# Two of eight token tiles of an expert mixture move from dense matmuls to gathered rows

## The reference

```python
experts = (i1 * PEER_NKEYS + i2).reshape(T, PEER_HEADS * K)
gates = jax.nn.softmax(top_s, axis=-1).reshape(T, PEER_HEADS * K)
...
a = jax.nn.gelu(jnp.einsum('td,ted->te', xb, u_tab[eb]), approximate=False)
coeff = (gb * a.astype(jnp.float32)).astype(xb.dtype)
return jnp.einsum('te,ted->td', coeff, v_tab[eb])
```

## Time and profile before

| what | value |
|---|---|
| median of three runs | 3731.43 us |
| span of the profiled execution | 3732.1 us |
| start of sweep 1, of sweep 2 (first matmuls) | 775.3, 2321.6 us |
| TensorE busy | 3570.5 us (96%) |
| DVE, ACT, POOL busy | 2290.6, 1202.6, 520.4 us |
| moved by DMA | 556.75 MB |

### The profile page before, as it was taken

How to read it: one execution, slowest core, us unless ns; L and a number is a source line. 1 busy time by engine, 2 the same in 40 slices (tenths; PEclk the granted TensorE clock), 3 DMA queues, 4 the chain that set the end, 5 groups by cost and what they waited for, 6 DMA issues and landing times. The chain is left out here.

```text
span 3732.1 us, 47838 instructions
## 1 busy us (share of the span) xinstructions
PE 3570.5 (96%) x16504; PEld 2955.7 (79%) x16504; DVE 2290.6 (61%) x3828; ACT 1202.6 (32%) x1342; POOL 520.4 (14%) x277
## 2 busy tenths in 40 slices
PE   4984999989999999999999999999999999999998
PEld 3862687878888888888888887888888878888887
DVE  5336243578988888888888844444444454444444
ACT  3123342123333333333333333222222232222222
POOL 0000000022333333333323332000000010000000
PEclk9995599999999999999999999999999999999999
DMA  6400022223333333333333333656655565565563
GB/s 245 157 27 23 15 105 90 84 72 141 135 141 139 140 140 137 138 140 135 136 139 136 138 132 138 235 190 198 242 188 192 196 209 191 188 199 188 189 198 139
DMA packets 223303, 556.75 MB, mean 149 GB/s; under 512 B 16528, under 2 KB 105744, under 8 KB 221072
## 3 DMA queue, kind: packets, MB, share of 16 engines
q1 hardware_dynamic: 222384, 552.88, 42.0%
q0 software_dynamic: 864, 3.15, 0.2%
HBM read 404.96 MB, written 150.99 MB: 149 GB/s over the span
## 5 line engine op out<-in xcount | busy, mean ns | idle before, releaser
L77 DVE TENSOR_TENSOR v_lo<-v_raw,v_hi 128x1024 fp32r<-128x1024 f32 x256 | 317.1, 1239 | 763.6 <-ACT v_hi L72 763.6
L1318 POOL TENSOR_TENSOR onehot<-onehot,slots 128x1024 fp32r<-128x1024 f32 x256 | 482.7, 1906 | 1349.5 <-DVE onehot L1378 1349.5
L1622 PE MATMUL y_ps<-v_hi,c_hi 128*128 128x512 f32 x2048 | 632.1, 390 | 10.7 <-DVE c_lo L77 9.3
L87 PE MATMUL acc_u<-a_hi,u_hi 128*128 128x512 f32 x2048 | 635.0, 391 | 3.6 <-PEq L1085 2.5
L87 PE MATMUL acc_u<-a_lo,u_hi 128*128 128x512 f32 x2048 | 632.8, 390 | 0.0
L87 PE MATMUL acc_u<-a_hi,u_lo 128*128 128x512 f32 x2048 | 632.2, 390 | 0.0
L1622 PE MATMUL y_ps<-v_lo,c_hi 128*128 128x512 f32 x2048 | 631.5, 390 | 0.0
L1622 PE MATMUL y_ps<-v_hi,c_lo 128*128 128x512 f32 x2048 | 631.2, 389 | 0.0
L72 ACT ACTIVATE v_hi<-v_raw 128x1024 fp32r<-128x1024 f32 x256 | 271.6, 1061 | 979.4 <-PE y_ps L1622 976.6
L1622 PEld LDWEIGHTS y_ps<-v_hi,c_hi 128*128 128x128 f32 x2048 | 384.5, 188 | 92.2 <-DVE v_lo L77 9.8
L87 PEld LDWEIGHTS acc_u<-a_lo,u_hi 128*128 128x128 f32 x2048 | 385.5, 188 | 81.5
(11 more groups left out here) (212 smaller groups left out, 3407.3 us busy)
## 6 DMA issues: line engine op xcount, KB each, us to landing
v_raw<-in_v SPq DMA_DIRECT2D x256, 512.0 KB, 5.3
u_raw<-in_u SPq DMA_DIRECT2D x128, 512.0 KB, 3.2
act_d<-gelu SPq DMA_DIRECT2D x128, 512.0 KB, 2.6
gate_d<-gate_block SPq DMA_DIRECT2D x16, 4096.0 KB, 12.1
gt<-gate_d SPq DMA_DIRECT2D x64, 1024.0 KB, 7.8
at<-act_d SPq DMA_DIRECT2D x256, 256.0 KB, 4.6
w_mod_b<-in_w_mod SPq DMA_DIRECT2D x6, 2560.0 KB, 8.9
w_mod<-in_w_mod SPq DMA_DIRECT2D x9, 1024.0 KB, 16.4
```

The lines of the kernel that those rows point to most:

```text
L77: return dve.tensor_tensor(lo, raw, hi.bitcast(F32), ALU.subtract)
L87: done = pe.matmul(acc[:, cols], w, a[:, k, cols], start=first, stop=last)
L1318: last = pool.tensor_tensor(onehot_2[u][:, :, part, :], onehot_2[u][:, :, 0, :].bitcast(F32), gate.unsqueeze(2).to_broadcast([P, TOK // 2, ...
L1622: done = pe.matmul(yps[t][:, cols], c, v[s][:, cols], start=first and k == 0, stop=last and k == 2)
```

## The change

Token tiles 0 to 5 stay dense, three a round. Tiles 6 and 7 (SPARSE = 2) get no gate matrix and no part in the matmuls of sweep 2. Sweep 1 still computes act_d for all tokens. It now takes nine steps for each dense tile: eight with gates, and a closing one in which the softmax of the next tile is normalised and its slots are read; then eight steps with only top-k (late_step), one more closing step and a last one, 64 in all. For tiles 6 and 7 the closing step keeps the gates (picked_gates), the number of each chosen expert (eidx) and the address of its activation (aidx).

In sweep 2 POOL issues for each of the 256 choices (128 a tile) two indirect DMAs: one picks one activation for each of the 128 tokens (4 bytes each) into a column of picked_act, the other fetches the chosen row of v for each token (128 rows of 4 KB) into one of eight row buffers. A fetch waits until the row sum that last used its buffer is done. DVE multiplies eight columns of gates and activations at a time (coefficients) and adds each row, times its coefficient, to one of two partial sums (add_row). From the second group of eight expert tiles on there is one row after each expert tile; the first group of the second round takes two a tile. POOL's additions and stores of the first round come in its queue after row 152. At the end the two sparse tiles are finished on ACT and DVE and stored by SP. The semaphores of the first stage are cleared by SP at the start of the projections and used again.

The core of the diff:

```diff
+SPARSE = 2
+DENSE = TT - SPARSE
+DTOK = DENSE * P
+CHOSEN = HEADS * TOPK
+TILE_STEPS = HEADS + 1
+STEPS = NKEYS // 2
...
+ROUNDS = 2
+RT = DENSE // ROUNDS
+WIDTH = RT * P
+BLOCKS = WIDTH // GTOK
...
     if s % GROUP == 0:
-        per = HALF // GTOK
-        gates = g.gate_d[r * per:(r + 1) * per, :, bass.ds(n, GROUP), :]
+        gates = g.gate_d[r * BLOCKS:(r + 1) * BLOCKS, :, bass.ds(n, GROUP), :]
         sp.dma_start(g.gt[s // GROUP][:], gates.rearrange("j p n t -> p j n t")).then_inc(g.gt_in[s // GROUP], 16)
-    sp.dma_start(g.act_in[s % RING][:], g.act_d[n][:, r * HALF:(r + 1) * HALF]).then_inc(g.act_in_sem[s % RING], 16)
+    sp.dma_start(g.act_in[s % RING][:], g.act_d[n][:, r * WIDTH:(r + 1) * WIDTH]).then_inc(g.act_in_sem[s % RING], 16)
     sp.dma_start(g.v_raw[s % RING][:], g.i["v"][n]).then_inc(g.v_in[s % RING], 16)
...
+def chosen_rows(g, dve, s):
+    flat = lambda a: a.rearrange("p a b -> p (a b)")
+    dve.scalar_tensor_tensor(g.eidx[:, s, :], flat(g.chosen[:, 1]), float(NKEYS), flat(g.chosen[:, 0]), ALU.mult, ALU.add)
+    dve.drain()
+    dve.tensor_scalar(g.aidx[:, s, :], g.eidx[:, s, :], float(S), g.token_col[:, s:s + 1], ALU.mult, ALU.add)
+    dve.tensor_tensor(g.picked_gates[:, s, :].rearrange("p (h k) -> p h k", k=TOPK), g.gates[:],
+                      g.norm[:].unsqueeze(2).to_broadcast([P, HEADS, TOPK]), ALU.mult)
+    dve.drain()
...
+                close(j)
+            if opening is not None:
+                opening()
+                tile(0, 1)
+            with eng.Fori(0 if opening is None else 1, DENSE - 1) as j:
+                tile(j)
+            tile(DENSE - 1)
+            with eng.Fori(0, HEADS - 1) as h:
+                late_step(h, False)
+            late_step(HEADS - 1, True)
+            close(DENSE)
+            last_step()
...
+            def close(j):
+                p = TILE_STEPS * j + HEADS
+                norm_topk(g, dve, j + 1, g.exps)
+                if isinstance(j, int) and j >= DENSE - 1:
+                    dve.wait_ge(onehot_ready, 2 * HEADS * DENSE)
+                    chosen_rows(g, dve, j - DENSE + 1)
+                    dve.sem_inc(picked, 1)
+                    split(2 * (p + 1), 0)
+                else:
+                    scale_gates(g, dve, g.slots_ready)
+                    split(2 * (p + 1), 0)
+                    dve.wait_ge(onehot_ready, 2 * HEADS * (j + 1))
...
+            def close(j):
+                product(TILE_STEPS * j + HEADS, 0)
+                if not (isinstance(j, int) and j >= DENSE - 1):
+                    pe.wait_ge(gate_out, 2 * HEADS * (j + 1) + 1)
+                    pe.wait_ge(g.slots_ready, j + 2)
                     transpose_slots()
...
+    cf = [g.at(f"cf{s}", 104 + 2 * s, [P, WIDTH]) for s in range(2)]
+    c_hi = [g.at(f"c_hi{s}", 108 + 2 * s, [P, WIDTH], F32R) for s in range(2)]
     y = g.at("y", 64, [P, RT, D])
     x1 = g.at("x1", 128, [P, TT, D])
...
+            def pick_acts(turn):
+                if turn >= 2:
+                    pool.wait_ge(picked_in[turn % 2], UNROLL * 16 * (turn // 2))
+                for e in range(turn * UNROLL, (turn + 1) * UNROLL):
+                    pool.indirect_dma_start(out=picked_act[:, e:e + 1], out_offset=None, in_=act_table,
+                                            in_offset=bass.IndirectOffsetOnAxis(ap=index(g.aidx, e), axis=0))\
+                        .then_inc(picked_in[turn % 2], 16)
+            def fetch_row(e):
+                if e >= UNROLL:
+                    pool.wait_ge(rows_done, e - UNROLL + 1)
+                pool.indirect_dma_start(out=rows[e % UNROLL][:], out_offset=None, in_=v_table,
+                                        in_offset=bass.IndirectOffsetOnAxis(ap=index(g.eidx, e), axis=0))\
+                    .then_inc(rows_in[e % UNROLL], 16)
...
+            def add_and_store(r, t, done):
+                n = r * RT + t
+                pool.wait_ge(y_scaled, n + 1)
+                pool.tensor_tensor(y[:, t, :], y[:, t, :], x1[:, n, :], ALU.add).then_inc(out_ready, 1)
+                pool.wait_ge(out_ready, done + 1)
+                pool.dma_start(g.out[n * P:(n + 1) * P, :], y[:, t, :]).then_inc(out_stored, 16)
...
+            for s in range(SPARSE):
+                for m in range(2):
+                    last = pool.memset(ys[s][m][:], 0.0)
+            last.then_inc(ys_zero, 1)
+            pick_acts(0)
             done = 0
-            for r in range(ROUNDS):
-                for t in range(RT):
-                    if by_pool(r, t):
-                        n = r * RT + t
-                        pool.wait_ge(y_scaled, n + 1)
-                        pool.tensor_tensor(y[:, t, :], y[:, t, :], x1[:, n, :], ALU.add).then_inc(out_ready, 1)
-                        done += 1
-                        pool.wait_ge(out_ready, done)
-                        pool.dma_start(g.out[n * P:(n + 1) * P, :], y[:, t, :]).then_inc(out_stored, 16)
+            for e in range(SPARSE * CHOSEN):
+                if e % UNROLL == 0 and e // UNROLL + 1 < TURNS:
+                    pick_acts(e // UNROLL + 1)
+                fetch_row(e)
+                late = e - (CHOSEN + 3 * UNROLL)
+                if late >= 0 and late % 4 == 0 and late // 4 < RT:
+                    if late == 0:
+                        pool.wait_ge(x1_in, 16)
+                    add_and_store(0, late // 4, done)
+                    done += 1
+            for t in range(RT):
+                if by_pool(ROUNDS - 1, t):
+                    add_and_store(ROUNDS - 1, t, done)
+                    done += 1
             pool.wait_ge(out_stored, done * 16)
         @block.scalar
...
+            def finish_sparse(s):
+                n = DENSE + s
+                act.wait_ge(ys_sum, s + 1)
+                act.activation(junk[:], ys[s][0][:], ACT.Square, accum_out=g.ssq[:, n:n + 1]).then_inc(ys_ssq, 1)
+                act.wait_ge(ys_ssq, s + 1)
+                act.activation(g.rstd[:, n:n + 1], g.ssq[:, n:n + 1], ACT.Sqrt, scale=1.0 / D, bias=g.eps[:]).then_inc(ys_root, 1)
...
+            def coefficients(turn, parity, count):
+                dve.wait_ge(picked_in[parity], UNROLL * 16 * count)
+                if not isinstance(turn, int) or turn:
+                    dve.wait_ge(rows_done, UNROLL * turn)
+                cols = bass.ds(UNROLL * turn, UNROLL)
+                dve.tensor_tensor(coef[:], picked_act[:, cols], picked_flat[:, cols], ALU.mult).then_inc(coef_r, 1)
+                dve.wait_ge(coef_r, turn + 1)
+            def add_row(turn, k, part):
+                dve.wait_ge(rows_in[k], (turn + 1) * 16)
+                if not isinstance(turn, int) or turn or k >= 2:
+                    dve.wait_ge(rows_done, UNROLL * turn + k - 1)
+                sums = ys[part][k % 2][:]
+                dve.scalar_tensor_tensor(sums, rows[k][:], coef[:, k:k + 1], sums, ALU.mult, ALU.add).then_inc(rows_done, 1)
...
+            def finish_sparse(s):
+                n = DENSE + s
+                dve.wait_ge(ys_root, s + 1)
+                dve.reciprocal(g.rstd[:, n:n + 1], g.rstd[:, n:n + 1])
+                dve.drain()
+                dve.scalar_tensor_tensor(ys[s][0][:], ys[s][0][:], g.rstd[:, n:n + 1], g.gate_rows[:, 1, :],
+                                         ALU.mult, ALU.mult).then_inc(ys_scaled, 1)
+                dve.wait_ge(ys_scaled, s + 1)
+                dve.tensor_tensor(ys[s][0][:], ys[s][0][:], x1[:, n, :], ALU.add).then_inc(ys_ready, 1)
...
+            for n in range(UNROLL):
+                step(0, 0, n)
+            dve.wait_ge(ys_zero, 1)
+            coefficients(0, 0, 1)
+            for s in range(UNROLL):
+                step(0, 1, s)
+                add_row(0, s, 0)
+            with dve.Fori(1, N // UNROLL // 2) as q:
+                for odd in range(2):
+                    turn = 2 * q - 1 + odd
+                    coefficients(turn, 1 - odd, q if odd == 0 else q + 1)
                     for s in range(UNROLL):
-                        prepare(base + UNROLL * q + s, s, base // RING + q * (UNROLL // RING) + s // RING + 1,
-                                base // UNROLL + q + 1)
-            for t in range(RT):
-                finish(ROUNDS - 1, t)
+                        step(0, 2 * q + odd, s)
+                        add_row(turn, s, 0)
+            first = N // UNROLL - 1
+            for n in range(UNROLL):
+                step(1, 0, n)
+                if n >= 2 and n - 2 < RT:
+                    finish(0, n - 2)
+                turn = first + n // (UNROLL // 2)
+                if n % (UNROLL // 2) == 0:
+                    coefficients(turn, turn % 2, turn // 2 + 1)
+                for k in range(2 * n % UNROLL, 2 * n % UNROLL + 2):
+                    add_row(turn, k, turn * UNROLL // CHOSEN)
+            sum_sparse(0)
+            dve.wait_ge(x1_in, 16)
+            base = first + 2
+            coefficients(base, base % 2, base // 2 + 1)
+            for s in range(UNROLL):
```

(60 more changed lines are left out.)

283 lines of the change are left out of this document (155 added, 128 removed).

## The result

The kernel after takes 3410.98 us (median of four runs, 3409.18 to 3415.09), the kernel before 3731.58 beside it: ratio 0.914, 95% interval 0.913 to 0.916. The forecast was 3400 us in a range of 3345 to 3600.

What follows compares the result with a forecast made beforehand. The prediction took TensorE's matmul count as the bound, with transfers narrowly overtaking it in sweep 2 after the change. It summed 3732 - 348 - 34 + 38 + 6 + 6 = 3400 us, range 3345 to 3600.

Steps and rivals of the forecast that it cites:

- Matmuls, -348: Sweep 2: 18 matmuls an expert tile in place of 24, 4.08 us a step, saving 348 us if the rest keeps up.
- case C: Sweep 2: transfers are cheap and TensorE stays the bound, 3362 us; chance 0.64 together with the forecast.
- Gates, -34: Sweep 1: the last two tiles' gates are not built; 16 of 64 steps lose two groups of 1.05 us, saving 34 us.
- DVE, 0: Sweep 2: DVE's step with the new row sum takes 3.3 of 4.08 us, so cost 0.
- POOL's queue, 2 to 3 us a step: Sweep 2: two indirect DMAs a step take POOL 2 to 3 us, under 4.08, so cost 0.
- Rivals A and B: Sweep 2: A, shared port costs a little, 3490 to 3600 us, chance 0.20; B, POOL becomes the bound, 3978 us, 0.14.
- 3930 us: Kernel end if each indirect DMA beside DVE took the skill's 3100 ns, 6.2 us a step in sweep 2.
- Transfers, +38: Sweep 2: transfers narrowly overtake TensorE, 1074 or 1105 us against 1055; cost 38 us, bounds 0 and 242.
- the waits of a few tenths of a us per step: Sign in sweep 2: v_hi waiting on v_raw or DVE on its rows, with DMA share 0.9 or more.
- the picks' 51 us: Sweep 2 transfers: the 4-byte picks at 0.2 us each, 51 us in all, bounds 0 and 243.
- Between the rounds, +6: Sweep 2 hand-over: DVE sums two rows a step in round 2's first eight steps, 40.5 us against TensorE's 32.6; +6 us.
- Tail, +6: After the last matmul: two sparse tiles to finish; last store leaves about 21 us after it, not 15.3; +6 us.

Runs made afterwards that it cites:

- extra-bytes run: The mended tail run (3372.6 us) with 128 KB more per step loaded and not used: 3379.35 us.
- fastest version: The mended tail run with the eight extra rows of round 2's first eight steps spread over the 40 steps behind: 3361.22 us, ratio to before 0.901.
- x1 in pieces: The kernel after with x1 loaded in eight loads of 0.5 MB, one per eight steps, instead of one of 4 MB: 3411.62 us.
- paced picks: The kernel after with two picks and a row per step in the first eight steps, then one pick with each row: 3400.85 us.
- mended tail: The 3389.53 us version (paced picks, x1 in pieces) with first picks in order of use and POOL's last-round additions and stores moved to DVE and SyncE: 3372.6 us.
- rows only, x1 in pieces: The kernel after without the picks (coefficients from a buffer of ones) and with x1 loaded in eight pieces: 3376.4 us.

## Why the prediction was right, point by point

The total was right to 11 us of 3411. The mechanism of the gain was right; the term for the transfers came out by luck. Against the profiled span of 3413.2 the forecast is 13.2 us short: -4.2 in the gates, +12.9 in the holes (56.9 against 38 + 6) and +4.5 in the tail, which partly cancel.

**Matmuls, -348:** right. A steady step is 4.08 us, and the run without the gather, 3367.1, confirms the sum of 3362 for case C.

**Gates, -34:** -38.2 measured. From its first to its last product sweep 1 is 35.9 us shorter, 1.12 us for each of the 32 groups instead of 1.05; 0.8 us were gained ahead of it and 1.5 behind it.

**DVE, 0:** right. The row sum is 1.287 us, v_lo 1.236, and the run without the gather, which keeps all sums, has the steady step unchanged.

**POOL's queue, 2 to 3 us a step:** right. The means of 1.09 and 1.21 us with a gap of 0.30 each are 2.9 a step; back to back, as at 2284 to 2325 us, most take 0.94 + 0.30. Rivals A and B fall with it, and so does the 3930 us that the prediction worked out from the figure below: the vector engine is busy 325 of 390 us and the row DMA takes 1.09 us in the mean (one of the 256 took 2.96). The Trainium skill's 3100 ns beside a tensor_copy ("SBUF — State Buffer", "A bandwidth-pool intuition that's wrong (but worth ruling out)") does not come with tensor_tensor and scalar_tensor_tensor on fp32 tiles here; this case has no tensor_copy of that kind beside POOL and cannot say more.

**Transfers, +38:** the size came out by luck, the step failed. The forecast spread it over all steps as a DMA time of 4.2 to 4.3 us against 4.08. In the steady step there is nothing, and the waits of a few tenths of a us per step that were to show it are not there: TensorE has no gap at shares of 0.92 to 0.96, nor at 0.99 or 1.02, and case C is what the windows show. What failed was above all one input, the picks, priced at 0.2 us each like 128 packets of 256 B. In the run with picks alone, from 3000 to 3300 us, 68 of them take 0.5% of the engines' time (queue, packets, MB, share), which is 0.02 us each:

```profile
q0 software_dynamic: 2240, 0.04, 0.5%
```

Without the picks' 51 us the forecast's own sum is 1023 us, under TensorE's 1055, and by the rate of sweep 1 it is 1054: only the picks made the transfers overtake. The rates were nearly right. In the kernel after a steady step takes 0.96 of 4.08, 3.9 us of the engines, and the forecast has 1013 / 256 = 3.96 without picks and x1; the extra-bytes run keeps up 386 GB/s for 200 us, where the forecast saw 207 to 236 in the stretches of gt's 1 KB runs. And "a queue this full does not run without holes", on which the choice inside +19 to +50 rested, does not hold for the steady steps. The whole 39.6 us of round 1 lies in two holes: 22.8 idle us at the start and 11.0 at 2575, and what the clock costs behind them: the 99 matmuls in the first window would take 22.5 us at 0.227 and took 28.9, at a granted clock of 0.72. (The run without the gather also loses some 3 us of clock there, so the parts add up to slightly more than the difference.)

**What makes the holes.** Shown: the second hole is the 4 MB load of x1 ahead of SyncE's next loads, at full engines (it goes with the pieces: 531.6 to 521.3). The first needs the picks (it is gone without them, and present without rows, smaller), and goes with their bursts. It is not bandwidth: v_hi waits until 2328.44 for a v tile issued at 2285.16. By 2294 SyncE's queue had moved 2.24 MB, and its five loads issued from 2282.72 to 2285.16 hold 2.23 (0.79 of gates, twice 0.20 and twice 0.52), so the bytes of that tile had been moved 34 us before (DMA view of 2283 to 2294 us: queue, packets, MB, share):

```profile
q1 hardware_dynamic: 1368, 2.24, 58.6%
```

And from 2301.6 to 2305.6 and again from 2321.6 on the engines carry next to nothing (DMA view of 2296 to 2328 us, slices of 0.8 us):

```profile
GB/s 236 1 69 213 317 267 37 1 0 1 0 0 61 166 311 382 372 342 405 389 405 415 410 415 425 405 425 404 415 415 420 146 5 1 1 0 1 0 1 0
```

Not settled: why the tile is seen so late. A lateness like it stands at the end, 7.6 to 8.9 us between the last byte of the software queue's store and the kernel's end, in all runs with indirect DMAs in which POOL stores last and not in the one without, and there it went with the queue. Whether both are one mechanism was not tried.

**Between the rounds, +6:** right. TensorE waits 9.6 us there against 3.1 before; the run with the rows spread takes 6 back. Behind it lies a cost that the forecast put at nothing when it passed over POOL's "three y additions and stores": the three additions now fall into the steady steps of round 2, and each holds up one operation of the vector engine, as in the earlier trace rows. For two of them (kernel after, POOL and DVE; the first usually takes 0.55 us, the second 1.23):

```profile
2939.47 2.62 POOL L1675 TENSOR_TENSOR y<-y,x 128x1024 f32<-128x1024 f32 x1
2939.74 2.76 DVE L1754 TENSOR_TENSOR cf<-gt,at 128x384 f32<-128x384 f32 x1
2949.42 2.41 POOL L1675 TENSOR_TENSOR y<-y,x 128x1024 f32<-128x1024 f32 x1
2949.82 3.10 DVE L83 TENSOR_TENSOR v_lo<-v_raw,v_hi 128x1024 fp32r<-128x1024 f32 x1 [0.77 <-ACT v_hi L78]
```

TensorE waits 2.0 us for it between 2900 and 3380 us here and 4.2 us in the fastest version, which still has these additions on POOL. No run moved them.

**Tail, +6:** +10.5. Two things were missed: the vector engine's y_part takes 3.37 us, not 1.28, beside POOL's addition, the exclusion that the earlier trace rows had shown; and from the end of POOL's last issue to the end of the kernel it is 9.5 us (3403.7 to 3413.2), before 4.0 (3728.1 to 3732.1). Together 7.6; the row work ahead of them was put some 3 us too long.

## What to carry to other kernels

A gather that fits into the steady step can still cost at its edges. Look at the first steps, at a big load in mid-sweep and at the hand-over, and spread there what comes in bursts: small gathers, large loads, doubled sums. Spreading gave about 40 us here, and the mended tail 10 more. An edit that gains nothing alone may still be worth its price once another one is in, as x1 in pieces was with paced picks, so try the pair before dropping either. And when a pair of transfer terms is summed against an engine's time, ask the trace for the best rate held over a long stretch as well as for the mean of the nearest rows.

## What was not expected of the hardware

- An indirect DMA costs POOL about the same for 128 rows of 4 KB (1091 ns in the mean, 937 at least) and for 128 elements of 4 B (1208 and 943). Bytes do not set it; whether the number of indices does was not tried.
- ACT waited up to 24.5 us for a load of SyncE's queue, beginning near the end of a burst of sixteen picks on POOL's and ending 3 us after the next eight, with the DMA engines idle for part of that time and the load's bytes moved long before.
- Runs of one kernel spread over 6 to 18 us with bursts of picks beside rows, 4 with bursts and no rows, 0.6 and 3 us without picks, 4 to 8 us with paced picks and double rows, and 0.7 us in the last version, with paced picks and rows spread.
- The DMA engines held 370 GB/s for 220 us (rows only, x1 in pieces) and 386 for 200 us (more bytes) with no gap in TensorE.
